# Decode values of a hybrid attention step: four batches at a time on four column groups

## The reference, cut to what matters

```python
o_c = einsum('bkgqc,bckd->bqkgd', p_c, vc)     # 32 compressed blocks
o_s = einsum('bkgqns,bkqnsd->bqkgd', p_s, gv)  # 1024 cached rows + the new one
o_w = einsum('bkgqw,bwkd->bqkgd', p_w, vw)     # the last 512 rows + the new one
o = gates_0 * o_c + gates_1 * o_s + gates_2 * o_w
y = x + o @ w_nsa_out
```

## Time and profile before

| | us |
|---|---|
| median of 3 runs | 1485.93 (1485.88 to 1487.59) |
| the profiled execution: its own time | 1487.97 |
| its span, first to last instruction | 1485.9 |
| TensorE busy with matmuls | 1450.8 |
| VectorE busy | 314.9 |
| ScalarE busy | 186.1 |
| mean granted TensorE clock | 0.992 of full speed |

### The profile page before, as it was taken

One profiled execution on the slowest core, in us unless ns is written; L12 is line 12 of the kernel. 1 busy time (PEld: TensorE's weight loads), 2 busy tenths in 40 slices (PEclk: granted clock), 3 DMA queues, 4 the chain that ended last, 5 costly groups with the idle time before them and its releaser, 6 DMA issues.

```text
span 1485.9 us, 32242 instructions
## 1 busy us (share of the span) xinstructions
PE 1450.8 (98%) x14271; PEld 847.8 (57%) x14271; DVE 314.9 (21%) x783; ACT 186.1 (13%) x466; POOL 36.2 (2%) x55
## 2 busy tenths in 40 slices
PE   9999999999998999999998999999998999999997
PEld 7887878878875558535544336335444345335444
DVE  5123222233256881300010000000010110010101
ACT  3000000001033661100000001000010000000102
POOL 3000000001000001000000000000000000000000
PEclk9999999999999999999999999999999999999998
DMA  9967666436525655899999999999999999999993
GB/s 325 358 263 278 231 255 223 160 131 201 157 96 191 175 128 226 317 376 399 398 408 425 426 406 425 424 359 397 408 410 425 425 408 425 420 348 405 426 425 123
DMA packets 95187, 475.63 MB, mean 320 GB/s; under 512 B 10008, under 2 KB 35784, under 8 KB 70207
## 3 DMA queue, kind: packets, MB, share of 16 engines
q1 hardware_dynamic: 92919, 467.58, 80.4%
q0 software_dynamic: 2128, 5.99, 1.3%
HBM read 469.65 MB, written 12.71 MB: 325 GB/s over the span
## 4 chain that ended last, share of the span: by engine, by line
PE 90%; DMA 5%; DVE 2%; SPq 1%; ACT 1%; issue 1%; DVEq 0%; ACTq 0%
PE banks L1185 34%; PE banks L1252 15%; PE banks L776 14%; PE banks L794 7%; PE banks L843 5%; DMA ring<-in_w_moe_down 2%; PE banks L1114 2%; DMA ring<-in_w_moe_gate 2%; PE banks L1294 2%; PE banks L921 2%; PE banks L757 1%; PE banks L1195 1%; PE banks L1041 1%; PE banks L938 1%; DMA ring<-in_state_win 1%; DMA ring<-in_w_pool 1%
## 5 line engine op out<-in xcount | busy, mean ns | idle before, releaser
L1185 PE MATMUL banks<-ring,arena 128*32 128x512 f32 (+1 forms) x5376 | 520.9, 540 | 1.7 <-DMA ring<-in_w_moe_gate 1.6
L1185 PEld LDWEIGHTS banks<-ring,arena 128*32 128x32 f32 x5376 | 177.5, 110 | 315.0 <-issue 305.7
L1252 PE MATMUL banks<-ring,arena 128*32 128x256 f32 x4704 | 261.6, 381 | 12.8 <-DMA ring<-in_w_moe_down 9.2
L1252 PEld LDWEIGHTS banks<-ring,arena 128*32 128x32 f32 x4704 | 152.9, 110 | 113.9 <-DMA ring<-in_w_moe_down 13.4
L776 PE MATMUL banks<-hT,ring 128*128 128x264 f32 x896 | 202.6, 387 | 0.0
L776 PEld LDWEIGHTS banks<-hT,ring 128*128 128x128 f32 x896 | 169.3, 190 | 36.9 <-issue 8.4
L2020 DVE TENSOR_TENSOR xT<-banks,xT 128x264 f32<-128x264 f32 x56 | 24.2, 433 | 487.0 <-PE banks L1294 487.0
L794 PE MATMUL banks<-arena,ring 128*128 128x264 f32 x448 | 101.5, 387 | 0.0
L794 PEld LDWEIGHTS banks<-arena,ring 128*128 128x128 f32 x448 | 84.6, 190 | 19.2 <-issue 5.0
L843 PE MATMUL banks<-hT,ring 128*128 128x264 f32 x256 | 57.5, 386 | 0.0
L2039 DVE TENSOR_TENSOR arena<-arena,banks 128x512 f32<-128x512 f32 (+1 forms) x42 | 24.2, 618 | 149.3 <-PE banks L1185 149.3
(11 more groups left out here) (324 smaller groups left out, 864.8 us busy)
## 6 DMA issues: line engine op xcount, KB each, us to landing
ring<-in_w_moe_gate SPq DMA_DIRECT2D x64, 1792.0 KB, 15.5
ring<-in_w_moe_up SPq DMA_DIRECT2D x64, 1792.0 KB, 15.7
ring<-in_w_moe_down SPq DMA_DIRECT2D x32, 2048.0 KB, 19.7
ring<-in_w_moe_down SPq DMA_DIRECT2D x32, 1536.0 KB, 20.1
arena<-in_cache_kv SPq DMA_DIRECT2D x64, 256.0 KB, 8.1
ring<-in_cache_kv SPq DMA_DIRECT2D x128, 128.0 KB, 2.2
ring<-in_w_ffn_gate SPq DMA_DIRECT2D x7, 2048.0 KB, 13.3
ring<-in_w_ffn_up SPq DMA_DIRECT2D x7, 2048.0 KB, 13.5
```

The source lines that it names most:

```text
L1185: last = mm(banks[CT * q:CT * (q + 1), 2 * t + part, 0:PART_W[part]], xe[:, c, CT * t:CT * (t + 1)], w[:, at:at + PART_W[part]], start=(c ...
L1252: last = mm(banks[CT * q:CT * (q + 1), 6 + place // 2, 256 * (place % 2):256 * (place % 2 + 1)], mh[:, t, at:at + CT], w[:, r, 256 * h:256 ...
```

## The change

`decode_values` takes a quad of four batches, on four column groups (partitions 0, 32, 64, 96 of bank 6 for quad 0, of bank 7 for quad 1), and two chunks a step: steps 1 to 6 for quad 0, steps 10 to 15 for quad 1. The waits on the loaded values of all four batches stand at the quad's first step; the wait on `od_sb` is gone, since each quad has its own bank. ScalarE copies the four batches' rows out at steps 7 and 16, into another buffer (`odn`, now in the selected branch's scores, which are no longer needed). TensorE turns them at steps 8 and 17 (eight transposes), and VectorE places each quad with two copies of 64x32 in place of eight of 64x8, at steps 9 and 17. SyncE's order changes with it: batches 6 and 7 are both loaded after the fourth `od_ps`, and the output weights after them. (`QUAD_AT` also lists which step does which chunks.)

```diff
--- before.py
+++ after.py
@@ -285,7 +285,8 @@
 
 
         PR_f, PT_f = carve(ring[:, (Q_SLOT0 + 1) % NSLOT, :], 4 * 512, 4 * 512)
-        odn = sc_w[:, 0:2 * KVW].rearrange("p (b n) -> p b n", b=2)
+        odn = sc_s[:, 0:4 * KVW].rearrange("p (b n) -> p b n", b=4)
+        QUAD_AT = {1 + n: (0, (2 * n, 2 * n + 1)) for n in range(6)} | {10 + n: (1, (2 * n, 2 * n + 1)) for n in range(6)}
         PR = PR_f.rearrange("p (s r t) -> p s r t", s=4, r=2)
         PT = PT_f.rearrange("p (s t) -> p s t", s=4)
         pst = pst_f.rearrange("p (s n r) -> p s n r", s=4, n=4)
@@ -553,13 +554,11 @@
             for b in range(1, 6):
                 sp.wait_ge(kt_ps, 8 * (1, 2, 4, 5, 6)[b - 1])
                 values(b)
-            sp.wait_ge(od_ps, 1)
+            sp.wait_ge(od_ps, 4)
             values(6)
+            values(7)
             for n in range(2):
-                sp.wait_ge(od_ps, n + 2)
                 out_tile(n)
-            sp.wait_ge(od_ps, 4)
-            values(7)
 
             def expert_tile(i, kind, k, weights):
 
@@ -1019,35 +1018,34 @@
                             if r == 1 and t == i:
                                 last.then_inc(pv_done, 1)
 
-            def decode_values(pair, quarter):
-
-                both = (2 * pair, 2 * pair + 1)
-                for b in both:
-                    if quarter == 0:
+            def decode_values(quad, cs):
+
+                bs = range(4 * quad, 4 * quad + 4)
+                outs = [banks[CT * x:CT * x + NH, 6 + quad, 0:KVW] for x in range(4)]
+                hs = [slice(NH * b, NH * (b + 1)) for b in bs]
+                if cs[0] == 0:
+                    for b in bs:
                         pe.wait_ge(vb_in[V_BUF[b]], vb_value(b))
-                        if pair >= 2:
-                            pe.wait_ge(od_sb, 2 * pair - 2)
-                outs = [banks[32 * (b % 2):32 * (b % 2) + NH, 6 + pair % 2, 0:KVW] for b in both]
-                hs = [slice(NH * b, NH * (b + 1)) for b in both]
-                if quarter == 0:
                     for r, kind in enumerate((VS_, VW_)):
-                        for x in range(2):
-                            mm(outs[x], PnT[0:TS, r, hs[x]], kvs[0:TS, kind * KVW:(kind + 1) * KVW], start=(r == 0), stop=False)
-                    for x, b in enumerate(both):
-                        mm(outs[x], PcT[0:NCMP_D, hs[x]], vcn[b][0:NCMP_D, :], start=False, stop=False)
-                for c in range(3 * quarter, 3 * quarter + 3):
-                    for x, b in enumerate(both):
+                        for x in range(4):
+                            mm(outs[x], PnT[0:TS, r, hs[x]], kvs[0:TS, kind * KVW:(kind + 1) * KVW], start=(r == 0), stop=False,
+                               skip_group_check=True)
+                    for x, b in enumerate(bs):
+                        mm(outs[x], PcT[0:NCMP_D, hs[x]], vcn[b][0:NCMP_D, :], start=False, stop=False, skip_group_check=True)
+                for c in cs:
+                    for x, b in enumerate(bs):
                         prob = PsT[:, c, hs[x]] if c < 8 else PwT[:, c - 8, hs[x]]
-                        last = mm(outs[x], prob, vbuf[b][:, c * KVW:(c + 1) * KVW], start=False, stop=(c == 11))
+                        last = mm(outs[x], prob, vbuf[b][:, c * KVW:(c + 1) * KVW], start=False, stop=(c == 11),
+                                  skip_group_check=True)
                         if c == 11:
                             last.then_inc(od_ps, 1)
 
-            def decode_outputs(pair):
-                for b in (2 * pair, 2 * pair + 1):
-                    pe.wait_ge(od_nat, 2 * pair + 2)
+            def decode_outputs(quad):
+                pe.wait_ge(od_nat, 4 * quad + 4)
+                for x in range(4):
                     for a in range(2):
-                        at = KVW + 32 * (b % 2) + NH * a
-                        last = tr(banks[:, 6 + pair % 2, at:at + NH], odn[0:NH, b % 2, P * a:P * (a + 1)], ident[0:NH, 0:NH])
+                        at = KVW + 64 * x + 24 * a
+                        last = tr(banks[:, 6 + quad, at:at + NH], odn[0:NH, x, P * a:P * (a + 1)], ident[0:NH, 0:NH])
                     last.then_inc(odt_ps, 1)
 
             pe.wait_ge(pcT_sb, 1)
@@ -1071,13 +1069,14 @@
                         last = tr(banks[0:TS, 3, P * (r + 1):P * (r + 2)], pn[:, r, :], ident)
                     last.then_inc(pdt_ps, 1)
                     pe.wait_ge(pdt_sb, 5)
+                if p in QUAD_AT:
+                    decode_values(*QUAD_AT[p])
                 if 1 <= p < 17:
-                    decode_values((p - 1) // 4, (p - 1) % 4)
                     prompt_transposes(p - 1)
                 if p >= 2:
                     prompt_values(p - 2)
-                if p >= 5 and p % 4 == 1:
-                    decode_outputs(p // 4 - 1)
+                if p in (8, 17):
+                    decode_outputs(p // 17)
 
 
             for c in range(2):
@@ -1430,13 +1429,13 @@
                         if q >= 4:
                             act.wait_ge(pv_done, q - 3)
                         nc.scalar.copy(PT[:, q % 4, 0:width], banks[:, 2 + q % 2, 0:width]).then_inc(pt_sb, 1)
-                if p >= 4 and p % 4 == 0:
-                    for b in (p // 2 - 2, p // 2 - 1):
-                        rows = slice(32 * (b % 2), 32 * (b % 2) + NH)
-                        act.wait_ge(od_ps, b + 1)
-                        if b >= 2:
-                            act.wait_ge(odt_ps, b - 1)
-                        nc.scalar.copy(odn[0:NH, b % 2, :], banks[rows, 6 + (b // 2) % 2, 0:KVW]).then_inc(od_nat, 1)
+                if p in (7, 16):
+                    quad = p // 16
+                    act.wait_ge(od_ps, 4 * quad + 4)
+                    if quad:
+                        act.wait_ge(odt_ps, 4)
+                    for x in range(4):
+                        nc.scalar.copy(odn[0:NH, x, :], banks[CT * x:CT * x + NH, 6 + quad, 0:KVW]).then_inc(od_nat, 1)
             def rows_out(hf, j):
 
                 nc.scalar.copy(xn[0:TT, j, 512 * hf:512 * (hf + 1)], banks[0:TT, 1 + j, :]).then_inc(xn_act, 1)
@@ -1878,16 +1877,15 @@
                     m = (p - 3) // 2
                     dve.wait_ge(pv_done, 4 * m + 4)
                     V.tensor_copy(hT[:, m, 0:TP], banks[:, m % 2, 0:TP]).then_inc(o_sb, 1)
-                if p >= 5 and p % 4 == 1:
-                    for b in (p // 2 - 2, p // 2 - 1):
-                        dve.wait_ge(odt_ps, 2 * (b // 2) + 2)
-                        for k2 in range(2):
-                            half = slice(HD * k2, HD * (k2 + 1))
-                            at = KVW + 32 * (b % 2)
-                            v = banks[half, 6 + (b // 2) % 2, at:at + 48].rearrange("p (a x) -> p a x", a=2)
-                            last = V.tensor_copy(hT[half, :, TP + b].rearrange("p (a g) -> p a g", a=2),
-                                                 v[:, :, GQA * k2:GQA * (k2 + 1)])
-                        last.then_inc(od_sb, 1)
+                if p in (9, 17):
+                    quad = p // 17
+                    dve.wait_ge(odt_ps, 4 * quad + 4)
+                    turned = banks[:, 6 + quad, KVW:KVW + 4 * 64].rearrange("p (b a x) -> p a x b", b=4, a=2)
+                    for k2 in range(2):
+                        half = slice(HD * k2, HD * (k2 + 1))
+                        last = V.tensor_copy(hT[half, :, TP + 4 * quad:TP + 4 * quad + 4].rearrange("p (a g) b -> p a g b", a=2),
+                                             turned[half, :, GQA * k2:GQA * (k2 + 1)])
+                    last.then_inc(od_sb, 4)
             for c in range(NC):
                 dve.wait_ge(wo_ps, c + 1)
                 tt(xT[:, c], banks[:, 4 + c % 3, 0:T], xT[:, c], ALU.add).then_inc(wo_added, 1)
```

## The result

The changed kernel takes 1494.72 us in the median of 8 runs, the kernel before 1486.28 in 8 runs. In a second set of runs it came to 1.0043 (1.0026 to 1.0059), 6.4 us (3.9 to 8.8). The forecast was 6.1 us slower. The profiled execution took 1492.68 us, with a span of 1490.5.

A forecast was written before the change was run, and what follows sets the result against it. The prediction took VectorE to pace the stage from 484 to 557 us. Net 4.2 us from late batch 7, 0.3 at the stage's end and 1.6 for the clock made 6.1 us slower, 1492.0 us; range 1486.0 to 1495.5.

The forecast's parts named there:

- The clock: TensorE's granted clock halves behind the wait at step 10, counted as 1.6 us from an earlier 2.16 us wait.
- rival 1: Shorter wait at step 10, clock that holds, low stretch at 585 us gone: 1.4 us slower, 1487.3 us; chance 0.14.
- The rate: Decode-value matmuls at 56 instead of 117 ns, 14.6 us less TensorE work, none counted in the steps VectorE paces.
- rival 4: The four column groups don't run side by side, matmuls stay at 117 ns: 1495.4 us; chance 0.04.
- rival 3: TensorE is the pace: 14.6 us come off, 1471.3 us, or about 1484 with late values; chance 0.04.
- Issue and landing: Batch 6 issued from 507.5, batch 7's last part at 525.0, landing 5.1 us later; TensorE waits 7.5 us at step 10.
- Behind the wait: Work queued from batch 7's landing to maximum 11 takes 5.4 us, so that maximum starts 5.5 us later than before.
- rival 5: Clock stays low until maximum 11 is fed: 5.4 us of work take 5.4 more, not 1.6; 1495.8 us; chance 0.04.
- the end of the stage: After VectorE's last weights, output copies and eight transposes make L1114 start 0.3 us later, besides the shift.
- The rule on transposes: Transposes not counting as clock activity would let the low clock outlast the wait; the row at 455 to 459 us spoke against.
- the 4 us: Sign of being wrong: TensorE's wait at step 10, forecast as some 7 us, turns out under 4 us.
- Nowhere else: Sign in the profile after: VectorE idle about 5 us or more ahead of one wide maximum only.

The follow-up runs named there:

- less_pe: Kernel before, with the first two of three chunks of every step of the decode values left out; ratio to before 0.9985.
- fill_fit: Changed kernel plus idle matmul calls: one in each of steps 7, 8, 9 and 16, seven at step 10 ahead of the wait; ratio to before 1.0024.
- fill_steps: Changed kernel plus three idle matmul calls in each of steps 7, 8, 9 and 16; ratio to before 1.0023.
- no_late: Changed kernel, with products of batches 6 and 7 reading the loaded values of batches 4 and 5, so no data is late at step 10; ratio to before 0.9984.
- quad_4_10: Changed kernel with the first quad at three chunks a step in steps 1 to 4, the second still at 10 to 15; ratio to before 0.9989.
- quad_later: Changed kernel with the second quad one step later, steps 11 to 16; ratio to before 0.9998.
- quad_4_6: Changed kernel with the first quad at three chunks a step in steps 1 to 4, the second at steps 11 to 16; ratio to before 0.9993.

## Why the prediction was right, and where it was off

**The direction and the mechanism** were right: slower, by the late batch 7 at step 10, with VectorE's pace swallowing the cheaper matmuls. Measured were 7.9 us against 6.1: inside the range, at the upper end of the forecast's own (3.0 to 8.0). That it stayed inside was in part luck. The clock cost some 3.5 us more than was counted, and 1.6 us came back in the output projection, where the low stretch of the earlier trace rows is missing; the prediction had named that only as a part of rival 1.

**The rate.** 56 ns was taken; the values of step 10 took 2.4 us for 40, 60 ns, and those of step 2 at full clock 0.99 us for 16, 62 ns. So rival 4 is out. less_pe took 15 us from TensorE and the stage shrank by 0.7, so the 14.6 us were worth next to nothing there, as counted; rival 3 is out.

**Issue and landing.** Counted from maximum 1, batch 6 was forecast to start at 21.5 us (507.5 - 485.97) and does at 21.4 (509.08 - 487.72), the last part of batch 7 at 39.0, and is at 39.1. It landed 3.7 us later in the first profile and 5.2 in the second; 5.1 was taken. In the second profile the wait is 7.36 us, forecast 7.5, and ends 44.0 us after maximum 1, forecast 44.1. In the first it is 3.90 us, since TensorE came 2.3 us later and the data 1.1 us sooner.

**Behind the wait**, at full clock: forecast 5.4, fill_fit 5.6. From maximum 11 to 15: forecast 17.2, measured 17.1.

**The step that was mis-sized is the clock.** "A wait of 7.5 us will hardly do less, so I count 1.6 us": a lower bound was taken as the price. It came to 3.7 to 3.9 us, since the low clock lasted for nearly 8 us of work behind the wait, 531.98 to 539.8 in the second profile, not for the 3.2 us of the earlier trace rows. That is nearly what rival 5 described. Rival 5 had priced it at 5.4 us, the clock being low until maximum 11 is fed; it came back shortly before, and the scores for that maximum (L984, 1.13 us) ran at the full clock. And the end of the stage lost another 1.35 us to the clock (10.47 us instead of 9.12), which was no term of the sum: step 16 has no values any more, TensorE idles 2.4 us there, and the clock fell in both profiles of the changed kernel. At full clock the end is 0.14 us longer than before, where 0.3 was counted. The low clock in steps 8 and 9 was not foreseen either, and was hidden behind the wait.

With these the first profile's sum closes: 42.87 (landing) + 9.50 - 44.04 = 8.33 us at maximum 11; 17.10 - 18.50 = -1.40 to maximum 15; 10.47 - 8.98 = 1.49 at the end; together 8.42, and 1.6 off for the low stretch of the projection that this execution did not have (51.1 against 49.5 us, above): 6.8 us. By the forecast: 5.5, -1.3, 0.3 and 1.6 for the clock.

**The rule on transposes.** I had set the row of 455 to 459 us against what the Trainium skill says in "TensorE: Matmul & The Clock Gate", Part 4, that transposes do not count as activity for the clock in the same way. Behind the wait the low clock went on through values and transposes alike, and in the changed kernel it came back while prompt values ran. This would fit the rule. Against it, the clock of fill_steps came back at about 535.4 us, while the last transposes ran and before any prompt values did. No run takes the transposes out, so the rule stays open, and so does what decides when the clock falls: the same idle time of 2.43 us at step 16 lowered it in the changed kernel and not in no_late or quad_4_10.

**What a profile after was to show.** The wait with state_win as its releaser, half the clock behind it, VectorE's long idle time ahead of a wide maximum: all there. "Some 7 us" holds for the second profile only. The 3.90 us of the first is under the 4 us that I had named as a sign of being wrong. That sign was badly chosen: the length of the wait depends on when TensorE comes as well, and the low clock of steps 8 and 9 had delayed it; the loss hangs on the end of the wait, 42.9 and 44.0 us after maximum 1. "Nowhere else" was wrong in the first profile, where VectorE idled 2.1 us at step 9 as well.

## What to carry to other kernels

When work is regrouped so that more of it shares a first step, ask for each buffer when it is now released and when its next content is now wanted; between the two must lie the whole chain of issue and landing (here 9.3 us of issuing a batch, two batches, and up to 5.2 to land). A faster engine that does not set the pace turns its gain into idle time, and on TensorE idle time can halve the clock just where the critical work resumes: price a wait as the wait plus the slow work behind it. And a schedule fixed by hand has cheap remedies: moving one quad by one step won back the loss (0.9998, 0.9986 to 1.0009).

## What the runs showed that was not expected

- The low clock behind the 7.36 us wait outlasted the resumption of work by 7.8 us; behind the 2.16 us wait of the earlier trace rows by 3.2 us. In quad_later, behind a wait of 0.99 us (and one of 1.49 us in the step before), TensorE worked for 2.2 us at the full clock before the clock fell; it was back at 536.3 us.
- TensorE's clock also falls without a long wait: in steps 8 and 9 of the changed kernel no idle time was longer than 1.5 us, and from 518 to 525 us the granted clock was 0.53. With idle matmuls in those steps it stayed at 1.00 in all five profiles that had them; without, it fell in one of the two profiles of the changed kernel, in no_late, quad_4_10 and quad_4_6, and not in quad_later.
- The last part of a batch, 512 KB, with the output weights issued right behind it, landed in 3.7 us in one execution of the changed kernel and in 5.2 in another.
